# RG-LRU gates as four 64 by 64 products on quarters of the array, with the input gate's halves swapped and swapped back

## The reference

```
xc, _ = causal_dwconv(u_lru, prev, w_lconv, b_lconv)          # width 4
r = sigmoid(block_diag(xc, w_a, b_a))                          # 16 blocks of 64 x 64
i = sigmoid(block_diag(xc, w_i, b_i))
log_a = -8 * r * softplus(-lam);  a = exp(log_a)
bterm = sqrt(1 - a*a) * i * xc
h[t] = a[t] * h[t-1] + bterm[t]                                # over 1024 frames, and 32 more
br_lru = (h * gelu(y_lru)) @ w_br_lru
```

## Time and profile before

| | |
|---|---|
| runs | 1793.26, 1793.29 and 1799.24 us, median 1793.29 us |
| profiled execution | 1792.71 us, of which the span from first to last instruction is 1790.9 us |
| granted TensorE clock | 1.000 over the span |
| PE busy | 1777.0 us (99%) |
| DVE, ACT, POOL busy | 841.1, 561.3, 494.5 us (47%, 31%, 28%) |
| recurrent stage, eight rounds | first visit at 489.7 us, last at 684.6 us |

### The profile page before, as it was taken

How to read it: one execution, slowest core, us unless ns; L and a number is a source line. 1 busy time by engine, 2 the same in 40 slices (tenths; PEclk the granted TensorE clock), 3 DMA queues, 4 the chain that set the end, 5 groups by cost and what they waited for, 6 DMA issues and landing times.

```text
span 1790.9 us, 29796 instructions
## 1 busy us (share of the span) xinstructions
PE 1777.0 (99%) x11192; PEld 1721.9 (96%) x11192; DVE 841.1 (47%) x1626; ACT 561.3 (31%) x1120; POOL 494.5 (28%) x280
## 2 busy tenths in 40 slices
PE   8999999999999999999999999999999999999999
PEld 7998888899999999999999999999999999999999
DVE  7967667511266765113464555312555511555511
ACT  5546544300176674112132333101233200333300
POOL 2121111222333232332233222333332233333222
PEclk9999999999999999999999999999999999999999
DMA  4021010111111111111411111111111111111113
GB/s 163 27 50 32 25 35 25 36 51 47 43 46 38 53 41 36 47 47 47 144 40 43 47 47 47 37 45 48 47 47 47 47 41 41 47 47 47 47 47 122
DMA packets 33090, 90.15 MB, mean 50 GB/s; under 512 B 7536, under 2 KB 12944, under 8 KB 33040
## 3 DMA queue, kind: packets, MB, share of 16 engines
q1 hardware_dynamic: 25664, 82.34, 14.1%
q10 hardware_dynamic: 7376, 7.09, 1.4%
HBM read 83.70 MB, written 4.73 MB: 49 GB/s over the span
## 4 chain that ended last, share of the span: by engine, by line
PE 95%; DVE 3%; ACT 1%; DMA 0%; issue 0%; ACTq 0%; SPq 0%; DVEq 0%
PE banks L449 86%; PE banks L601 2%; PE banks L564 1%; PE banks L531 1%; PE banks L587 1%; PE banks L780 1%; PE banks L781 1%; PE banks L541 1%; DVE x_lo L1280 1%; DVE sqsum L1288 0%; DMA resid<-xT 0%; DVE merged L1288 0%; DVE x_lo L1265 0%; ACT sqsum L1002 0%; DVE resid L1273 0%; ACT pr L978 0%
## 5 line engine op out<-in xcount | busy, mean ns | idle before, releaser
L449 PE MATMUL banks<-x_hi,w_hi 128*128 128x352 f32 x1752 | 578.3, 330 | 4.7 <-DVE x_lo L1265 3.0
L449 PE MATMUL banks<-x_hi,w_lo 128*128 128x352 f32 x1752 | 567.0, 324 | 0.0
L449 PE MATMUL banks<-x_lo,w_hi 128*128 128x352 f32 x1752 | 565.1, 323 | 0.0
L419 POOL TENSOR_SCALAR w_hi<-w_raw 128x1024 fp32r<-128x1024 f32 x136 | 153.6, 1130 | 1216.9 <-DMA w_raw<-W 1216.9
L449 PE MATMUL banks<-h_hi,w_lo 128*128 128x352 f32 x1152 | 372.7, 323 | 0.0
L449 PE MATMUL banks<-h_hi,w_hi 128*128 128x352 f32 x1152 | 372.4, 323 | 0.0
L449 PE MATMUL banks<-h_lo,w_hi 128*128 128x352 f32 x1152 | 371.6, 323 | 0.0
L449 PEld LDWEIGHTS banks<-x_hi,w_hi 128*128 128x128 f32 x1752 | 330.0, 188 | 10.4 <-issue 3.5
L421 POOL TENSOR_TENSOR w_lo<-w_raw,w_hi 128x1024 fp32r<-128x1024 f32 x136 | 332.1, 2442 | 11.4
L449 PEld LDWEIGHTS banks<-x_lo,w_hi 128*128 128x128 f32 x1752 | 329.5, 188 | 3.0
L449 PEld LDWEIGHTS banks<-x_hi,w_lo 128*128 128x128 f32 x1752 | 329.0, 188 | 0.0
(11 more groups left out here) (211 smaller groups left out, 1838.6 us busy)
## 6 DMA issues: line engine op xcount, KB each, us to landing
w_raw<-W SPq DMA_DIRECT2D x137, 512.0 KB, 3.4
sqsum<-xT ACTq DMA_DIRECT2D x2, 2112.0 KB, 13.8
o_yT<-resid SPq DMA_DIRECT2D x7, 528.0 KB, 5.1
resid<-xT SPq DMA_DIRECT2D x4, 704.0 KB, 9.8
resid<-xT SPq DMA_DIRECT2D x4, 352.0 KB, 5.6
w_raw<-W SPq DMA_DIRECT2D x4, 256.0 KB, 5.2
wabs<-wab ACTq DMA_DIRECT2D x8, 128.0 KB, 2.1
o_yT<-resid SPq DMA_DIRECT2D x3, 176.0 KB, 1.8
```

Source lines behind the costliest of these rows:

```text
L419: nc.gpsimd.tensor_scalar(w_hi[s][:, :], w_raw[s][:, :], 1.0, 0.0, ALU.mult, ALU.add).then_inc(w_hi_done, 1)
L449: last = nc.tensor.matmul(out[:, 0:cn], w[s if wt is None else wt][:, k * P:(k + 1) * P], x[:, k, cc:cc + cn], start=(k == 0 and j == 0), ...
```

## The change

PE's visit makes four products of 64 by 64 blocks in place of two of 128 by 128. Each takes 64 partitions of `XC` and 64 columns of the weight, so each occupies one quarter of the array, and the four quarters are different ones. The recurrence gate's two blocks (m = 0) lie on the diagonal and go to bank 6. The input gate's two (m = 1) lie off the diagonal: the block of partitions 0 to 63 writes partitions 64 to 127 of bank 7, and the other way round. The waits are followed by an increment of a semaphore that nothing else waits for. ACT takes the input gate out with two instructions of 64 partitions each, which also move the halves back. The input gate's bias is rolled by 64 on the host.

```
@@ lru_gates (PE)
-                nc.tensor.matmul(bank[6][:, 0:cn], wabs[:, 0, :], XC[n][:, 0:cn], start=True, stop=True)
-                nc.tensor.matmul(bank[7][:, 0:cn], wabs[:, 1, :], XC[n][:, 0:cn], start=True, stop=True).then_inc(r_ps, 1)
+                pe.sem_inc(s_own[1], 1)
+                for m in range(2):
+                    for e in range(2):
+                        of, to = slice(HD * e, HD * e + HD), slice(HD * (e ^ m), HD * (e ^ m) + HD)
+                        last = nc.tensor.matmul(bank[6 + m][to, 0:cn], wabs[of, m, of], XC[n][of, 0:cn], start=True, stop=True)
+                last.then_inc(r_ps, 1)
@@ lru_decay (ACT)
-                A(FI[:, ck], bank[7][:, 0:cn], ACT.Tanh, bias=halfb[:, cols(j + 3 * KT, 1)], scale=0.5).then_inc(r_tanh, 1)
+                for e in range(2):
+                    here, there = slice(HD * e, HD * e + HD), slice(HD - HD * e, P - HD * e)
+                    last = A(FI[here, ck], bank[7][there, 0:cn], ACT.Tanh, bias=halfb[there, cols(j + 3 * KT, 1)], scale=0.5)
+                last.then_inc(r_tanh, 1)
@@ host
-                 b_a=_cols(x["b_lru_a"][0]), b_i=_cols(x["b_lru_i"][0]), lam=_cols(x["lru_lambda"][0]),
+                 b_a=_cols(x["b_lru_a"][0]), b_i=np.roll(_cols(x["b_lru_i"][0]), HD, axis=0), lam=_cols(x["lru_lambda"][0]),
```

## The result

The change takes 1804.9 us (median of 7 runs, 1803.01 to 1807.41) against 1793.26 us of the kernel before beside it: ratio 1.0062, 95% interval 1.0053 to 1.0071. That is 0.62% slower. The time is 5.2 us above the forecast of 1799.7, inside the range of 1790 to 1808, but above the 1797.5 to 1802.0 of the forecast's own sum, and just outside the "within 0.5%" that had the highest chance. The profiled execution took 1805.34 us against 1792.71, its span 1803.2 us against 1790.9.

What follows compares the result with a forecast made beforehand. PE was taken as the bound, 26.72 us a round, just over an ACT and DVE ring that becomes 27.65. Rounds 1 to 6 5.6, round 0 0.2, eighth 0.65: sum 6.4, median offset 0.6, forecast 1799.7, range 1790 to 1808.

Steps and rivals of the forecast that it cites:

- within 0.5%: Whole kernel: the time would come within 0.5% of the kernel before, about 9 us; chance 0.69.
- What bounds the kernel: Recurrent stage: PE sets the 26.72 us round; the ACT and DVE ring without its two waits would take 26.0.
- PE's visit: PE, each of 24 visits: four quarters at once cut it from 1.18 to 0.93 us, 6.0 us in all.
- two at a time: Rival, PE's quarters: only two run together, visit 1.52 us, round 27.74, total 1801.5; chance 0.13.
- ACT's extra instruction: ACT, each chunk: the second `FI` instruction adds 0.45 us, between bounds of 0.22 and 0.55.
- The edit's rival at half the price: ACT's halves cost 0.22 each, ring 26.67, PE's old pace, about 1793 us; chance 0.07.
- What the two waits take up: ACT's ring, before the third `FA` and second `XC`: waits of 0.28 and 0.45 absorb 0.73 of the extra 0.90.
- The weight split: POOL's `w_hi` and `w_lo` against DVE's product and scans: 0.3 us more a round, between nothing and 0.6.
- The second lock: Rival: from a ring of 27.9, POOL's `w_hi` precedes the third `d_lo`, adding 1.05 every round, about 1808; chance 0.15.
- Round 0: First round of the recurrent stage: costs 0.2 us, between -0.25 for the shorter first visit and +0.62.
- The eighth round: Last round, PE already waiting for `FI`: two extra ACT instructions less the visit's gain, 0.90 - 0.25 = 0.65 us.
- The signs: Recurrent stage trace: PE idle about 1.5 us a round, first `FA`s 27.3 to 28 apart, two `FI` rows 0.45 apart.

Runs made afterwards that it cites:

- The control: Kernel before, with ACT's tanh of `FA` waiting for `FA` by its own semaphore instead of for `FI`: 1792.73 us, ratio 0.9997.
- the run with the swap left standing: The change, but one ACT instruction takes out the swapped input gate and nothing swaps it back, so it meets wrong channels: 1789.16 us, ratio 0.9973.
- the diagonal form: The change, but all four quarter products on the diagonal, no swap, one ACT `FI` instruction as in the kernel before: 1800.77 us, ratio 1.0046.
- DVE's swap: The change, but in rounds 0 to 6 ACT writes `FI` in one instruction and DVE's product with `XC` swaps back in two halves: 1797.16 us, ratio 1.0023.
- the last run: The change with DVE swapping, a separate `FA` wait, the eighth round as before, and quarters only in chunks 1 and 2 of rounds 0 to 6: 1789.85 us.
- `FA`'s own wait in the change: The change, but ACT's tanh of `FA` waits for `FA` by its own semaphore, no longer for `FI`'s two halves: 1800.19 us, ratio 1.0041.
- halves of columns: Kernel before, but ACT takes the input gate out with two instructions of 128 partitions and 176 columns each: 1796.95 us in its one execution.

## Why the prediction was right, and where it was off

- **What bounds the kernel** was right. PE bound it by a small margin over a ring of ACT and DVE, and the change made the ring the bound. The control (no gain from a shorter ring) and the run with the swap left standing (PE's gain in full in its trace) show both halves.
- **PE's visit** was right: 0.95 against 0.93 forecast, four quarters at once, and two banks shared by quarters of different rows. Its reason was not quite right: two products have each half of the rows, so what each has to itself is its quarter, not its rows and columns. The rival "two at a time" was priced right too, at 1.53 and 1800.8 (1.52 and 1801.5), but it belongs to the diagonal form.
- **ACT's extra instruction** is the term that was mis-sized. The step took "0.45, since both halves keep the columns of the row". It measured 0.68, above the upper bound of 0.55 that the step gave. A full instruction costs 0.45 because it overlaps its predecessor by 0.1; the second half doesn't (0.55), and another 0.12 is lost beside it. The edit's rival at half the price, 0.22, fell.
- **What the two waits take up** was read as 0.73 and is 0.93, which worked the other way. Together: 3 x 0.68 - 0.93 = 1.11 for the first half of the ring, against 3 x 0.45 - 0.73 = 0.62.
- **The weight split** was right in size, 0.29 against 0.3, and in most rounds in its course: `w_hi` waits for the product and then holds up the scan, `w_lo` the short scan. The size was in part luck: the step itself says that 0.1 us of position decides it, and 0.3 was the middle of its span. The second lock, on `d_lo`, did not come, though the ring passed the 27.9 from which it was to decide. That bound was wrong by the step's own figures: the third `d_lo`, 0.52 long, starts 0.87 before the end of a round, so a `w_hi` at 27.57 stands in front of it only from 28.4 on. In the change `w_hi` comes at 27.71 to 27.88 of rounds 1 to 6, behind the third `d_lo`'s start at 27.23 to 27.38.
- **Round 0** was to cost between -0.25 and 0.62. It costs the ring 1.51, about as much as rounds 1 to 5 (1.39 to 1.54): 1.09 ahead of the product and 0.41 behind it. PE's first visits do follow each other 0.24 closer, but that is spent at the first wait.
- **The eighth round**, 0.65 forecast, was two halves less the visit's own gain. That is what it was, 1.35 - 0.24 = 1.1, with halves of 0.68. The 1.4 for the clock was not foreseen. That the clock fell because of the two holds is argued from the rows: it fell behind them in the change (1.96 and 2.01 us) and with DVE's swap (1.82 and 2.01), and not where they were 1.51 and 1.94.
- **The signs** came in kind and not in size: PE's idle in front of the visits is 1.9 us a round against 1.5, ACT's first `FA`s stand 28.0 to 28.2 apart in rounds 1 to 6 against 27.3 to 28, and the two `FI` rows 0.56 against 0.45.

In sum: 6.4 forecast; 2.6 more in rounds 1 to 6 (8.17 against 5.6), 1.3 in round 0, 0.4 and 1.4 in the eighth, and 0.1 ahead of the stage make 12.2 of the 12.3. So the mechanism was right and the loss nearly twice the forecast. That the time still lies in the range is luck: the range went up to 1808 for the second lock, and 1804.9 was reached without it.

## What to carry to other kernels

When PE bounds a loop by less than a microsecond a round, saving PE's time is worth only what the other engines' ring leaves, and an instruction added to that ring is paid in full once its slack is used up; measure the ring first, by comparing the starts of rows that wait with those that don't, since idle times alone understate the slack (0.73 for 0.93). Splitting an instruction by partitions doubled its time here, on ACT (0.55 to 1.10) and on DVE (0.52 to 1.05), so leave the data swapped if the rest allows it, or pay for the swap in some of the chunks only, as the last run did. Four quarter products ran together when each had a quarter of its own; two on the same quarter went one after the other.

## What the runs showed of the hardware that was not expected

- Two ACT instructions of 64 partitions over 352 columns take 0.55 us each and don't overlap each other; two of 128 partitions over 176 columns take 0.40 each and 0.70 together, and a full instruction starts 0.45 behind its predecessor.
- Four products on four different quarters start within 0.02 us of each other, though two of them with different rows write the two halves of one bank.
- The granted clock can fall for 3.4 us behind two waits of PE of some 2 us each, 5 us apart, and then takes matmuls from 0.16 to 0.29 us apart; the same stage without the fall had holds of 1.51 and 1.94. Such holds are not the only place: the trace with `FA`'s own wait in the change has a fall at 11.0 us, behind waits of PE of 1.22, 1.24 and 0.45, where the kernel before had 0.30, 0.99 and 0.45 and kept its clock, and the one with halves of columns has a fall at 131.8, behind a wait of 3.44.
